# One layer of a hybrid trunk: early U blocks as one stream of 120, with all their low halves on VectorE

## What is computed

```python
def peer_layer(h, w_q, keys_a, keys_b, expert_u, expert_v):
    q = (h @ w_q).reshape(t_tot, PEER_HEADS, PEER_QUERY_DIM)      # 8 heads x 256
    s1 = jnp.einsum('thd,hkd->thk', q1, keys_a)                   # 128 keys each
    s2 = jnp.einsum('thd,hkd->thk', q2, keys_b)
    v1, i1 = lax.top_k(s1, 16); v2, i2 = lax.top_k(s2, 16)
    top_s, pos = lax.top_k(sums of all pairs, 16)                 # of 16384 experts
    gates = softmax(top_s)
    act = gelu(einsum('td,thkd->thk', h, expert_u[idx]))
    y = einsum('thk,thkd->td', gates * act, expert_v[idx])
x = x + gate2 * y; return rms(x) * g_final
```

## Time and profile before

| | us |
|---|---|
| median of three runs | 1810.03 |
| the profiled execution | 1812.44 |
| its span | 1810.7 |
| PE busy in it | 1625.5 |
| DVE busy | 1379.5 |
| ACT busy | 655.4 |
| POOL busy | 605.6 |

### The profile page before, as it was taken

One profiled execution on the slowest core, in us unless ns is written; L12 is line 12 of the kernel. 1 busy time (PEld: TensorE's weight loads), 2 busy tenths in 40 slices (PEclk: granted clock), 3 DMA queues, 4 the chain that ended last, 5 costly groups with the idle time before them and its releaser, 6 DMA issues. The chain is left out here.

```text
span 1810.7 us, 24627 instructions
## 1 busy us (share of the span) xinstructions
PE 1625.5 (90%) x8101; PEld 1412.2 (78%) x8101; DVE 1379.5 (76%) x2650; ACT 655.4 (36%) x999; POOL 605.6 (33%) x439
## 2 busy tenths in 40 slices
PE   3899898888999952799978999999999999999995
PEld 2687655667989842799977888899999999999994
DVE  6773334647999999899955677777878888888888
ACT  2323464343433230344423333333333333333332
POOL 1241123225544331223211111134444445454452
PEclk8899899999999976799988999999999999999998
DMA  8463300004434220265449999999999999999984
GB/s 334 157 253 106 128 1 1 24 1 163 148 122 139 90 81 9 111 242 211 191 173 354 292 315 313 325 313 341 336 345 342 330 349 339 329 350 341 336 323 143
DMA packets 154042, 398.20 MB, mean 220 GB/s; under 512 B 12624, under 2 KB 78304, under 8 KB 150624
## 3 DMA queue, kind: packets, MB, share of 16 engines
q1 hardware_dynamic: 117088, 262.82, 41.3%
q0 software_dynamic: 36864, 134.23, 20.4%
HBM read 358.73 MB, written 38.27 MB: 219 GB/s over the span
## 5 line engine op out<-in xcount | busy, mean ns | idle before, releaser
L1535 ACT CAST v_hi<-v_raw 128x1024 fp32r<-128x1024 f32 x128 | 134.7, 1053 | 380.7 <-issue 359.1
L1524 POOL DMA_INDIRECT row<-in_u_rows,row_index x128 | 145.1, 1134 | 376.5 <-DVE row_dots L1630 336.4
L1738 PE MATMUL ps_y<-v_hi,w_hi 128*128 128x512 f32 x768 | 239.9, 393 | 8.5 <-DVE w_lo L1601 8.5
L997 POOL TENSOR_TENSOR u_lo_early<-u_raw_early,u_hi_early 128x1024 fp32r<-128x1024 f32 x56 | 150.1, 2696 | 272.4 <-ACT u_hi_early L992 272.4
L1742 PE MATMUL ps_y<-v_hi,w_lo 128*128 128x512 f32 x768 | 238.3, 392 | 0.0
L1740 PE MATMUL ps_y<-v_lo,w_hi 128*128 128x512 f32 x768 | 238.3, 391 | 0.0
L1524 POOL DMA_INDIRECT row<-in_v,row_index x128 | 174.9, 1366 | 177.5 <-DVE y_row L1648 158.7
L1624 DVE TENSOR_TENSOR v_lo<-v_raw,v_hi 128x1024 fp32r<-128x1024 f32 x128 | 156.4, 1222 | 69.0 <-ACT v_hi L1535 69.0
L1005 PE MATMUL ps_u_early<-h_hi,u_hi_early 128*128 128x384 f32 x448 | 156.6, 350 | 52.8 <-PEq L1024 33.1
L1726 PE MATMUL ps_a<-h_hi,u_lo 128*128 128x384 f32 x576 | 193.3, 336 | 0.0
L1724 PE MATMUL ps_a<-h_hi,u_hi 128*128 128x384 f32 x576 | 193.2, 335 | 0.0
(11 more groups left out here) (280 smaller groups left out, 3180.1 us busy)
## 6 DMA issues: line engine op xcount, KB each, us to landing
v_raw<-in_v SPq DMA_DIRECT2D x128, 512.0 KB, 5.7
u_raw<-in_u SPq DMA_DIRECT2D x72, 512.0 KB, 5.3
u_raw_early<-in_u SPq DMA_DIRECT2D x56, 512.0 KB, 5.1
w_ada<-in_w_ada SPq DMA_DIRECT2D x12, 2048.0 KB, 8.1
gate_tiles<-g_tile SPq DMA_DIRECT2D x12, 2048.0 KB, 6.4
gates<-gate_tiles SPq DMA_DIRECT2D x32, 768.0 KB, 10.2
activations<-u_act_early SPq DMA_DIRECT2D x56, 192.0 KB, 1.9
act<-activations SPq DMA_DIRECT2D x56, 192.0 KB, 5.4
```

The costliest lines, as they stand in the source:

```text
L1524: pool.indirect_dma_start(out=row[q % GS][:], out_offset=None, in_=table[q // PICKS], in_offset=bass.IndirectOffsetOnAxis(ap=rows["index"] ...
L1738: pe.matmul(out, hi, v_hi[i % VS][:, c], start=first, stop=False)
```

## The change

`BlockProducts` becomes `UpProducts`: one stream of all 128 U blocks with one ring of four raw, high and low buffers and two PSUM banks. VectorE makes every low half, two blocks ahead of TensorE; ScalarE splits three ahead, SyncE loads six ahead. Blocks 0 to 79 run in retrieval (6 in the first turn, 14 in the last, 10 in the others, `TURN_START`), 80 to 119 in `dense_gates`, 120 to 127 at the opening of `experts`, ahead of the first V block. In a turn TensorE does the next head's query after its second and third block and the scores after its fourth.

`PickedRows` holds the row work, now with eight buffers. `h_row` is made at the start of retrieval; the 128 dots run in retrieval (68, from the second turn on, `DOTS_BY`) and in the gates (60); the experts stage fetches only rows of V and adds one in each iteration. GpSimd has its subtracts of the query weights and the fetches. VectorE places u_lo and dots between the steps of the top-k by the shares given to `settle` and `beside`. All loops are written out. In the experts stage all activations come from DRAM, and buffers that were apart share space.

The diff, cut to its core (`settle` stands after each step of the turn, with 0.52, 0.58, 0.64, 0.67, 0.7, 0.73, 0.84, 0.93 and 1.0 in those left out):

```diff
-FILL = 4
-EARLY_BLOCKS = 2
-FILLED = FILL * (PEER_HEADS + G_TILES // 2)
-GROUP = 8
-N_GROUPS = N_KEYS // GROUP
+ROW_READS = 2 * PICKS
+TURN_START = [0, 6, 16, 26, 36, 46, 56, 66, 80]
+DOTS_BY = [0, 0, 8, 18, 28, 38, 48, 58, 68]
+GATED = 120
...
+    RING, LEAD, AHEAD, DEEP = 4, 2, 3, 6
...
+    def load(self, sp, b):
+        n = b % self.RING
+        if b >= self.RING:
+            sp.wait_ge(self.lo_done, b - self.RING + 1)
+        sp.dma_start(self.raw[n][:], self.io["u"][b]).then_inc(self.u_in[n], 16)
+
+    def high(self, act, b):
+        n = b % self.RING
+        act.wait_ge(self.u_in[n], 16 * (b // self.RING + 1))
+        if b >= self.RING:
+            act.wait_ge(self.mul, b - self.RING + 1)
+            act.wait_ge(self.lo_done, b - self.RING + 1)
         act.copy(self.hi[n][:], self.raw[n][:]).then_inc(self.hi_done, 1)
 
-    def low(self, eng, i, n):
-        eng.wait_ge(self.hi_done, i * self.slots + n + 1)
-        wait_count(eng, self.mul, (i - 1) * self.slots + n + 1)
-        eng.tensor_tensor(self.lo[n][:], self.raw[n][:], self.hi[n][:].bitcast(F32), ALU.subtract).then_inc(self.lo_done, 1)
-
-    def product(self, pe, i, n):
-        h_hi, h_lo = self.keep["h_hi"], self.keep["h_lo"]
-        pe.wait_ge(self.lo_done, i * self.slots + n + 1)
-        wait_count(pe, self.act_done, (i - 1) * self.slots + n + 1)
+    def low(self, dve, b):
+        n = b % self.RING
+        dve.wait_ge(self.hi_done, b + 1)
+        if b >= self.RING:
+            dve.wait_ge(self.mul, b - self.RING + 1)
+        dve.tensor_tensor(self.lo[n][:], self.raw[n][:], self.hi[n][:].bitcast(F32), ALU.subtract).then_inc(self.lo_done, 1)
...
+    def product(self, pe, b):
+        h_hi, h_lo, n = self.keep["h_hi"], self.keep["h_lo"], b % self.RING
+        out = self.ps[b % 2][:, 0:DENSE]
+        pe.wait_ge(self.lo_done, b + 1)
+        if b >= 2:
+            pe.wait_ge(self.act_done, b - 1)
...
+    def vector_at(self, dve, b):
+        if b + self.LEAD < N_KEYS:
+            self.low(dve, b + self.LEAD)
+
+    def scalar_before(self, act, b):
+        if 0 < b <= N_KEYS:
+            self.gelu(act, b - 1)
+
+    def scalar_after(self, act, b):
+        if b + self.AHEAD < N_KEYS:
+            self.high(act, b + self.AHEAD)
+
+    def sync_at(self, sp, b):
+        if b + self.DEEP < N_KEYS:
+            self.load(sp, b + self.DEEP)
+        if b >= 2:
+            self.store(sp, b - 2)
...
+    def gather(self, pool, q):
+        n, j = q % self.RING, q % PICKS
+        pool.wait_ge(self.indexed, min(PEER_HEADS, q // TOPK + 1))
+        if q >= self.RING:
+            pool.wait_ge(self.row_used, q - self.RING + 1)
+            pool.wait_ge(self.row_in[n], 16 * (q // self.RING))
+        pool.indirect_dma_start(out=self.row[n][:], out_offset=None, in_=self.table[q // PICKS],
+                                in_offset=bass.IndirectOffsetOnAxis(ap=self.index[:, j:j + 1], axis=0))\
+            .then_inc(self.row_in[n], 16)
+
+    def dot(self, dve, q, h_row):
+        n = q % self.RING
+        dve.wait_ge(self.row_in[n], 16 * (q // self.RING + 1))
+        dve.tensor_tensor_reduce(self.row[n][:], self.row[n][:], h_row[:], 1.0, 0.0, ALU.mult, ALU.add, self.dots[:, q:q + 1])\
+           .then_inc(self.row_used, 1)
...
+            def query_low(h):
+                for s in range(2):
                     pool.wait_ge(wq_hi, h * 2 + s + 1)
-                    wait_count(pool, q_done, h * 2 + s - 1)
+                    pool.wait_ge(q_done, h * 2 + s - 1)
                     pool.tensor_tensor(w_lo[s][:], w[s][:], w_hi[s][:].bitcast(F32), ALU.subtract).then_inc(wq_lo, 1)
-                for n in range(FILL):
-                    fill.low(pool, h, n)
-
-            turns(pool, PEER_HEADS, turn)
-            for n in range(FILL):
-                fill.low(pool, PEER_HEADS, n)
+
+            for h in range(PEER_HEADS):
+                if h < LAST:
+                    pool.wait_ge(s_copied, 2 * h + 2)
+                    query_low(h + 1)
+                for r in range(gathered(h), gathered(h + 1)):
+                    rows.gather(pool, r)
...
+            for h in range(PEER_HEADS):
+                for t, b in ticks(h):
+                    up.product(pe, b)
+                    if h < LAST and Q_AT <= t < Q_AT + 2:
+                        query_of(h + 1, t - Q_AT)
+                    if h < LAST and t == S_AT:
+                        scores_of(h + 1)
...
+                def beside(share):
+
+                    while at[0] < TURN_START[h] + int(share * blocks):
+                        up.vector_at(dve, at[0])
+                        at[0] += 1
+                    while at[1] < DOTS_BY[h] + int(share * dots):
+                        if at[1] == 0:
+                            dve.wait_ge(h_kept, 2)
+                        rows.dot(dve, at[1], h_row)
+                        at[1] += 1
+
+                def settle(share):
+                    beside(share)
                     dve.wait_ge(chain, steps[0])
...
+                for s, b in both:
+                    note(dve.max(top[:, s, b, 0:8], scores[:, s, b]))
+                settle(0.1)
+                for s, b in both:
+                    note(dve.match_replace(rest[:, s, b], top[:, s, b, 0:8], scores[:, s, b], NEG))
+                    note(dve.max_index(idx[:, s, b, 0:8], top[:, s, b, 0:8], scores[:, s, b]))
+                    if (s, b) == (0, 3):
+                        beside(0.2)
+                settle(0.3)
                 dve.sem_inc(s_read, 1)
-                stage(dve.max(top[:, s, b, 8:16], rest[:, s, b]) for s, b in both)
-                stage(dve.max_index(idx[:, s, b, 8:16], top[:, s, b, 8:16], rest[:, s, b]) for s, b in both)
+                for s, b in both:
+                    note(dve.max(top[:, s, b, 8:16], rest[:, s, b]))
+                settle(0.38)
+                for s, b in both:
+                    note(dve.max_index(idx[:, s, b, 8:16], top[:, s, b, 8:16], rest[:, s, b]))
+                settle(0.46)
...
+                dve.tensor_copy(rows.index[:, h * TOPK:(h + 1) * TOPK], picked[:, 0]).then_inc(rows.indexed, 1)
+                note(dve.tensor_copy(expert[:, :, h * TOPK:(h + 1) * TOPK], picked[:]))
+                dve.wait_ge(chain, steps[0])
...
+            up.low(dve, 0)
+            up.low(dve, 1)
+            for h in range(PEER_HEADS):
+                turn(h)
+            gates_of(LAST)
...
+def gathered(h):
+
+    return 0 if h == 0 else min(ROW_READS, DOTS_BY[h] + PickedRows.RING)
...
+        def blocks_at(x):
+
+            left = GATED - FIRST - OPENING
+            return range(FIRST + OPENING + x * left // N_BATCH, FIRST + OPENING + (x + 1) * left // N_BATCH)
+
+        def dots_at(x):
+            left = PICKS - DOTS_BY[PEER_HEADS]
+            return range(DOTS_BY[PEER_HEADS] + x * left // N_BATCH, DOTS_BY[PEER_HEADS] + (x + 1) * left // N_BATCH)
 
         @block.gpsimd
         def _(pool):
-            def turn(r, after, last=False):
-                for n in range(0 if last else FILL):
-                    fill.low(pool, early(r + 1), n)
-
-            all_turns(pool, turn)
+            for r in range(gathered(PEER_HEADS), PICKS + rows.RING):
+                rows.gather(pool, r)
...
+            for x in range(N_BATCH):
+                n, t0 = x % HB, ROW_TOK + x * BATCH
+                if x >= HB:
+                    dve.wait_ge(g_done, (x - HB + 1) * FPB)
+                dve.tensor_tensor(hot_j[n][:], keep["iota"][:].rearrange("p (o j) -> p o j", o=1).broadcast_to([P, BATCH, P]),
+                                  cols[:, 1, t0:t0 + BATCH].rearrange("p (t o) -> p t o", o=1).broadcast_to([P, BATCH, P]),
+                                  ALU.is_equal).then_inc(hot, 1)
+                for o in range(BATCH):
+                    dve.tensor_scalar(hot_i[n][:, o], keep["iota"][:], cols[:, 0, t0 + o:t0 + o + 1], cols[:, 2, t0 + o:t0 + o + 1],
+                                      ALU.is_equal, ALU.mult).then_inc(hot, 1)
+                for b in blocks_at(x):
+                    up.vector_at(dve, b)
+                for r in dots_at(x):
+                    rows.dot(dve, r, h_row)
...
+            for b in range(FIRST, FIRST + OPENING):
+                up.scalar_before(act, b)
+                up.scalar_after(act, b)
+            for x in range(N_BATCH):
...
+                for b in blocks_at(x):
+                    up.product(pe, b)
...
+            for n in range(2):
+                sp.wait_ge(g_stored[n], 16 * (G_TILES // 2))
+            load_gates(0)
...
+            for i in range(-OPENING, N_KEYS):
+                if i < 0:
+                    up.sync_at(sp, N_KEYS + i)
+                    continue
...
+            for r in range(PICKS + rows.RING, ROWS):
+                rows.gather(pool, r)
...
+            for i in range(-OPENING, N_KEYS):
+                if i < 0:
+                    up.vector_at(dve, N_KEYS + i)
+                if i == -2:
```

(79 more changed lines are left out.)

597 lines of the change are left out of this document (234 added, 363 removed).

## The result

The changed kernel takes 1721.56 us (median of four runs, 1720.53 to 1724.61) against 1810.01 before: a ratio of 0.951, 95% interval 0.950 to 0.953. The prediction was 1736 with a range of 1703 to 1787. The profiled execution has a span of 1722.9 us.

The account below looks back on a forecast made before the run. Retrieval and gates were taken as bound by VectorE, experts by TensorE with DMA close behind. Gates' end 1138 + 33 + 5 + 544 + 14 = 1734 us span, 1733 as median, plus 3 for overlap: 1736, range 1703 to 1787.

Parts of the forecast that it names:

- Retrieval, 855: Retrieval stage: VectorE and TensorE nearly balanced, eight turns plus first gathers and close, ending at 855 us.
- A middle turn: Retrieval: 54.5 us on TensorE and 55.1 on VectorE, taken as 56 us a turn.
- Contention: Retrieval: 14 query-weight subtracts left on GpSimd still hold up VectorE, 28 us; waits behind the other subtracts go.
- Gates, 8 + 270: Dense gates: 8 us before the batches, then VectorE's 265 us leading TensorE's 249, plus 5.
- the 5 us for an uneven mix: Dense gates: 5 us added to VectorE's 265 for uneven work, making 270.
- Gathers beside one-hots at nothing: Dense gates: new gathers cost VectorE's one-hot operations 0 us; the other end was 56 us.
- Hand-over, 5: End of gates: last U product, 4 us, and hand-over to experts, 1 us.
- Experts, V loop, 4.25 us a block: Experts: DMA at 339 GB/s sets 1.442 MB per V block, 4.25 us each, 544 us for all 128.
- The rival that DMA hides: Experts: V loop keeps 4.08 us a block as queues can exceed 339 GB/s; 1714 us, chance 0.12.
- Tail, 14: End of experts: 13.6 us from the last matmul to the end, entered as 14.
- The 3 us for imperfect overlap: Whole kernel: 3 us added because balanced engines seldom overlap as well as sums say.
- Lockstep: Retrieval and gates: rings don't carry the imbalance, VectorE and TensorE wait on each other; up to 1887 us, chance 0.08.

Follow-up runs that it names:

- e2: e1, but GpSimd makes the query low half of head 2 ahead of the eight first gathers in the first turn; 1713.21 us.
- e5: Changed kernel with a one-column memset in place of each of the 128 dots of gathered U rows, gathers and waits kept; 1692.22 us.
- e3: Changed kernel with the low halves of the early U blocks (retrieval and gates) back on GpSimd; 1829.35 us, ratio 1.010.
- e7: Kernel before the change, with only its 56 early U low halves moved from GpSimd to VectorE; 1816.3 us, ratio 1.0026.
- e1: Changed kernel with the last four gathers of the gates stage issued only in experts; 1719.18 us, ratio 0.9495.
- e4: Changed kernel with 131 KB more loaded per V block, from block 4 on, into tiles that nobody reads; 1727.95 us.
- e9: Changed kernel with 393 KB more loaded per V block (124 of them) into spare tiles that nobody reads; 1792.65 us.
- e10: e2, with SyncE loading the gates after the first U stores in experts, and first V and activation loads spread between those stores; 1701.78 us.
- e11: e10 with the last 16 row dots of the gates moved into the opening of experts; 1700.16 us, ratio 0.9379.

## Why the prediction was right, and where it was off

The span was forecast as 1734 and is 1722.9. By the steps of the sum:

- **Retrieval, 855: right, 859.** A middle turn was put at 56 us for two nearly tied engines and is 54.4, TensorE's own sum of 54.5. VectorE's sum of 55.1 was too high, since the middle turns from the fourth on do not take that long. The six middle turns together take 338.4 us where the forecast had 336, since one of them is long: the eight first gathers in front of the query's low half were given 4 us once, and the second turn is 11 us longer than the others. e2, which takes that order away, brings it to 54.3 us and makes the first one 3.8 longer, a net 7 of the 11. e5 keeps the order and leaves the dots out, and the second turn is 57.6: so most of the 11 us needs both, the gathers in front and the dots beside them; how they act together stays open. The first turn is 2.5 us shorter than forecast, the last 2 us longer. The turns start 2 us late, but in nine more traces, with the same code up to there, they start anywhere from 419.0 to 423.0: that is no error of the sum.
- **Contention.** The remaining query subtracts cost VectorE 4.5 us a turn, 4 by the sum, but TensorE bounds the middle turns, so they do not reach the end there. That GpSimd's subtracts held up VectorE was right, by the earlier trace rows and by e3 and e7.
- **Gates, 8 + 270: right, 6.5 + 265.3.** VectorE leads, and the 5 us for an uneven mix were not needed. TensorE's 249 is 239 in e5.
- **Gathers beside one-hots at nothing: right**, 2.12 to 2.14 us for eight with a gather beside them.
- **Hand-over, 5: wrong, 14.5.** The step counted the last U product and the block's end, and no DMA. Gathers are new in that stage, and GpSimd's queue did not pass the block's end before they had landed; e1 shows it (3.2 us without). The working had counted the moved gathers' issue, and not their landing.
- **Experts, V loop, 4.25 us a block: wrong, 4.08**, 22 us in all. The term took 339 GB/s at 95% share for a ceiling. But it was only what that loop asked for: e4 and e9 move 379 and 386. The rival that DMA hides had 0.12 and was the true case for this term. It gave 1714, and the other terms add the 8 us up to the measured time. The Trainium skill (DMA: Bandwidth & Descriptors, Specifications) gives about 358 GB/s from HBM as the limit of a core. The 379 of e4 and the 386 of e9 are above it, and the measurement decides; the changed kernel's 354 is a demand and tests no limit.
- **Tail, 14: right, 14.4.** The 3 us for imperfect overlap had no place to go.

Together: + 4 in retrieval, - 6 in the gates, + 9.5 at the hand-over, - 19 in experts (22 for DMA, less 3 in the opening), about - 11 on the span. Two errors of opposite sign, 9.5 and 22 us, thus stand behind a miss of 14 us on the median (3 of it the overlap term). That they partly cancel is luck. Lockstep did not come: from the fourth to the seventh turn VectorE waits 0.3 us in all for ScalarE's splits, and TensorE shows no wait.

What the runs do not take apart: the loops that are now written out, the activations that all come from DRAM and the shared buffers came in the same change, and no run has the hoisting of U blocks and dots alone. That low halves on VectorE are worth some 108 us inside the change is shown (e3), and that they are worth nothing without a new order is shown too (e7, as placed there); what the rest is worth is read from the windows.

The best versions, e10 and e11, take 1700 to 1702 us, 0.938 to 0.940 of the kernel before; so the changed kernel still held 20 us, in the hand-over, one GpSimd order and one SyncE order.

## What to carry to other kernels

A high DMA rate or share in a loop that another engine bounds is that loop's demand, not a limit: put more load beside it before a forecast charges for DMA. When work is moved into a stage, follow its transfers to the stage's end and to the next one's first queue entries, since here the gains of e1 and e11 were lost to the next wait behind them. And an engine that is relieved gives time only if the moved instruction's inputs are ready at its new place in the queue.

## What was not expected of the hardware

- The profile's DMA share goes past 1: 1.06 at 379 GB/s, 1.05 at 386; in a short stretch 414 GB/s at 1.03. At 1.00 (354 GB/s) there was room.
- At a block's end GpSimd's queue drained until its last gathers had landed: 6.9 us in e11, 10.9 in e1, 13.6 in the changed kernel, 14.9 in e4. In the changed kernel the last two gathers took 10.6 us to land, beside a 2 MB store, and the one before them 4.6.
- One VectorE subtract took 5.68 us instead of 1.22, beside two GpSimd subtracts of 4.75 us together: it was held through both.
